# Latent mixer of a hybrid encoder step: search steps settled by GpSimd, and sixteen transposed copies moved from ACT to DVE

## What is computed

```python
def mla_core(k_nope, k_rope, v, k_pos, q_nope, q_rope, q_pos):        # mixer B
    logits = einsum('bqhd,bshd->bhqs', q_nope, k_nope) + einsum('bqhd,bsd->bhqs', q_rope, k_rope)
    logits = where(chunk_mask(q_pos, k_pos), logits * 96 ** -0.5, -inf)
    return einsum('bhqs,bshd->bqhd', softmax(logits, axis=-1), v)

idx_score = where(chunk_mask(q_pos, k_pos), idx_score, -inf)          # mixer A
_, sel = lax.top_k(idx_score, 256)
```

## Time and profile before

| | |
|---|---|
| median of three runs | 3007.67 us |
| the profiled execution, its own time | 3008.22 us |
| its span, first to last instruction | 3006.4 us |
| mean granted TensorE clock | 0.978 |
| PE busy over the span | 2833.9 us (94%) |
| DVE busy | 2018.3 us (67%) |
| ACT busy | 1412.2 us (47%) |
| POOL busy | 532.4 us (18%) |

### The profile page before, as it was taken

One profiled execution on the slowest core, in us unless ns is written; L12 is line 12 of the kernel. 1 busy time (PEld: TensorE's weight loads), 2 busy tenths in 40 slices (PEclk: granted clock), 3 DMA queues, 4 the chain that ended last, 5 costly groups with the idle time before them and its releaser, 6 DMA issues. The chain is left out here.

```text
span 3006.4 us, 49479 instructions
## 1 busy us (share of the span) xinstructions
PE 2833.9 (94%) x18462; PEld 2368.9 (79%) x18462; DVE 2018.3 (67%) x3648; ACT 1412.2 (47%) x2850; POOL 532.4 (18%) x410
## 2 busy tenths in 40 slices
PE   8986997999999999899999899999899999999998
PEld 6762564668899999788799566865688999998787
DVE  5447999865867776677631565139857777767777
ACT  5335996552444344433243455348724444444333
POOL 0000222420011110465000231000000111114551
PEclk9996999999999999999999999999999999999999
DMA  4111001021233323654411201120112333326442
GB/s 154 46 36 29 14 14 50 2 65 67 75 97 104 107 97 96 235 172 129 168 51 46 92 2 53 56 77 2 58 74 61 101 109 99 104 91 227 154 130 103
DMA packets 203120, 259.04 MB, mean 86 GB/s; under 512 B 27100, under 2 KB 132180, under 8 KB 202900
## 3 DMA queue, kind: packets, MB, share of 16 engines
q1 hardware_dynamic: 202900, 256.10, 25.8%
HBM read 177.90 MB, written 77.64 MB: 85 GB/s over the span
## 5 line engine op out<-in xcount | busy, mean ns | idle before, releaser
L247 PE MATMUL X<-up_th,high 128*128 128x272 f32 x1232 | 356.4, 289 | 4.1 <-ACT up_U L2287 2.9
L249 PE MATMUL X<-up_th,low_r 128*128 128x272 f32 x1232 | 355.2, 288 | 0.0
L247 PEld LDWEIGHTS X<-up_th,high 128*128 128x128 f32 x1232 | 232.2, 188 | 8.3 <-ACT up_U L2287 6.1
L2248 POOL TENSOR_TENSOR up_sum<-up_U 128x512 f32<-128x512 f32 x20 | 33.4, 1669 | 1131.9 <-DVE up_U L2399 1131.9
L249 PEld LDWEIGHTS X<-up_th,low_r 128*128 128x128 f32 x1232 | 231.9, 188 | 0.0
L2381 DVE SCALAR_TENSOR_TENSOR up_cv<-up_G,tap,up_cv 128x1024 f32<-128x1024 f32 (+1 forms) x176 | 130.3, 782 | 136.9 <-ACT up_cv L2296 135.3
L247 PE MATMUL up_x<-up_th,up_high 128*128 128x272 f32 x704 | 202.9, 288 | 1.4 <-DVE up_low_r L1859 1.4
L249 PE MATMUL up_x<-up_th,up_low_r 128*128 128x272 f32 x704 | 203.7, 289 | 0.0
L248 PE MATMUL X<-sums_r,high 128*128 128x272 f32 x528 | 152.0, 288 | 0.0
L247 PE MATMUL up_y<-up_th,up_high 128*128 128x272 f32 x528 | 151.9, 288 | 0.0
L249 PE MATMUL up_y<-up_th,up_low_r 128*128 128x272 f32 x528 | 151.6, 287 | 0.0
(11 more groups left out here) (581 smaller groups left out, 8665.6 us busy)
## 6 DMA issues: line engine op xcount, KB each, us to landing
scratch_a<-up_U SPq DMA_DIRECT2D x44, 544.0 KB, 2.7
low<-in_w_up_dram SPq DMA_DIRECT2D x44, 512.0 KB, 5.1
up_low<-in_w_up_dram SPq DMA_DIRECT2D x44, 512.0 KB, 4.9
scratch_s<-up_sum SPq DMA_DIRECT2D x80, 256.0 KB, 2.0
b_f<-in_w_down_dram SPq DMA_DIRECT2D x40, 512.0 KB, 4.4
a_lo_p_f<-scratch_s SPq DMA_DIRECT2D x40, 512.0 KB, 4.2
a_lo_p_f<-scratch_a SPq DMA_DIRECT2D x30, 512.0 KB, 4.5
scratch_att<-out_x SPq DMA_DIRECT2D x16, 512.0 KB, 2.6
```

Of the source, the lines that this page charges most:

```text
L247: nc.tensor.matmul(out, lh, rh, start=first, stop=False, skip_group_check=on_top)
L249: return nc.tensor.matmul(out, ll, rh, start=False, stop=last, skip_group_check=on_top)
L2248: g.tensor_tensor(t0, a21, a22, ALU.add).then_inc(pair_summed, 1)
```

## The change

Two edits in `attention`, for mixer B alone.

The settling moves from DVE to POOL. POOL's loop scales unit i for both heads and then settles the steps of unit i. It works with a difference and a signed step `flip` (a power of two whose sign is that of the score) in place of a comparison, a predicated copy and an exclusive-or. A step other than the first issues six operations: limit minus count; whether that is at least zero; that times `flip`; the sum of `bits` and the product; half of `flip`; the sum of the two as the next candidate. Each of the first three is waited for before the next. DVE's two calls of `settle` go; before `next_float` it waits for the last settling.

The copy of group 1 of head 1, `(x, j) == (1, 1)`, moves from ACT to DVE. Only wide units have a group 1, so there are 16 such copies, of 128, 256, 384 and 512 columns. On DVE they stand first in the unit.

```diff
--- before.py
+++ after.py
@@ -977,7 +977,9 @@
 
         if what == "x":
             return "dve" if j % 2 else "act"
-        if mla or stick:
+        if mla:
+            return "dve" if (x, j) == (1, 1) else "act"
+        if stick:
             return "act"
         return "act" if x == 0 else "dve"
 
@@ -995,7 +997,8 @@
             below = sb("below", [P, wide[-1]], BF16)
             up = sb("up", [P, n_top], mybir.dt.int32)
             counted = {"dve": sem("counted_dve"), "act": sem("counted_act")}
-            settled, cand_ready = sem("settled"), sem("cand_ready")
+            flip = sb("flip", [P, n_top], mybir.dt.int32)
+            settled, cand_ready, flipped = sem("settled"), sem("cand_ready"), sem("flipped")
         if mla or dsa:
             top, work, spare, told = src["top"], src["work"], src["top"]["spare"], sem("told")
             scratch = below if mla else sb("scratch", [P, 2 * SEQ], BF16)
@@ -1094,6 +1097,31 @@
                     for h in range(2):
                         g.memset(left[s][h][:, SEQ:SEQ + 1], 1.0).then_inc(cleared, 1)
                 return
+            def settle(step):
+
+                for by, n in (("dve", BY_DVE), ("act", n_top - BY_DVE)):
+                    pool.wait_ge(counted[by], FROM + n * (step + 1))
+                room = top["ok"][:].bitcast(F32)
+                g.tensor_tensor(room, top["limit"][:], top["cnt"][:], ALU.subtract).then_inc(settled, 1)
+                pool.wait_ge(settled, FROM + 4 * step + 1)
+                if step:
+                    g.tensor_scalar(top["cand"][:], room, 0.0, None, ALU.is_ge).then_inc(settled, 1)
+                    pool.wait_ge(settled, FROM + 4 * step + 2)
+                    g.tensor_tensor(top["cand"][:], top["cand"][:], flip[:], ALU.mult).then_inc(settled, 1)
+                    pool.wait_ge(settled, FROM + 4 * step + 3)
+                    g.tensor_tensor(top["bits"][:], top["bits"][:], top["cand"][:], ALU.add).then_inc(settled, 1)
+                    if step + 1 < STEPS:
+                        g.tensor_scalar(flip[:], flip[:], 0.5, None, ALU.mult).then_inc(flipped, 1)
+                else:
+                    g.tensor_scalar(top["bits"][:], room, 0.0, 1.0, ALU.is_ge, ALU.subtract).then_inc(settled, 2)
+                    g.tensor_scalar(flip[:], room, 0.0, 2.0, ALU.is_ge, ALU.mult).then_inc(settled, 1)
+                    pool.wait_ge(settled, FROM + 4)
+                    g.tensor_scalar(flip[:], flip[:], 1.0, float(1 << 30), ALU.subtract, ALU.mult).then_inc(flipped, 1)
+                if step + 1 < STEPS:
+                    pool.wait_ge(settled, FROM + 4 * step + 4)
+                    pool.wait_ge(flipped, FROM + step + 1)
+                    g.tensor_tensor(top["cand"][:], top["bits"][:], flip[:], ALU.add).then_inc(cand_ready, 1)
+
             for i, (p, t) in enumerate(order):
                 n, w = queries(t), key_tile(t)[0]
                 for h in range(2):
@@ -1101,6 +1129,8 @@
                     c = 2 * (i % ring) + h
                     pool.wait_ge(rcp_done[h], FROM + i + 1)
                     g.tensor_scalar(pr, pr, rr[0:n, c:c + 1], 1.0, ALU.mult, ALU.mult).then_inc(prob_ready[h], 1)
+                for step in (SEARCH_AT[i] if mla else ()):
+                    settle(step)
 
         @block.tensor
         def _(pe):
@@ -1417,20 +1447,6 @@
                     v_.tensor_scalar(below[:, wide[j]:wide[j + 1]], w[:], top["cand"][:, j:j + 1].bitcast(F32), None, ALU.is_lt, ALU.add,
                                      accum_out=top["cnt"][:, j:j + 1]).then_inc(counted["dve"], 1)
 
-            def settle(step):
-
-                for by, n in (("dve", BY_DVE), ("act", n_top - BY_DVE)):
-                    dve.wait_ge(counted[by], FROM + n * (step + 1))
-                v_.tensor_tensor(top["ok"][:], top["cnt"][:], top["limit"][:], ALU.is_le).then_inc(settled, 1)
-                dve.wait_ge(settled, FROM + 2 * step + 1)
-                if step:
-                    v_.copy_predicated(top["bits"][:], top["ok"][:], top["cand"][:]).then_inc(settled, 1)
-                else:
-                    v_.tensor_scalar(top["bits"][:], top["ok"][:], 1.0, None, ALU.subtract).then_inc(settled, 1)
-                dve.wait_ge(settled, FROM + 2 * step + 2)
-                if step + 1 < STEPS:
-                    v_.tensor_scalar(top["cand"][:], top["bits"][:], 1 << (30 - step), None, ALU.bitwise_xor).then_inc(cand_ready, 1)
-
             def not_above(columns):
                 for j in columns:
                     w = work[SEARCHED[j]]
@@ -1517,8 +1533,6 @@
                 if i + ahead < n_units:
                     for h in range(2):
                         peak(i + ahead, h)
-                if mla and len(SEARCH_AT[i]) > 1:
-                    settle(SEARCH_AT[i][0])
                 if i:
                     pieces_of(dve, "dve", i, "x")
                     if not mla:
@@ -1531,9 +1545,8 @@
                     count_below(SEARCH_AT[i][-1])
                 if i + 2 < n_units:
                     over_sum(i + 2, 0)
-                if mla and SEARCH_AT[i]:
-                    settle(SEARCH_AT[i][-1])
                 if mla and i == SEARCH_ENDS + 1:
+                    dve.wait_ge(settled, FROM + 4 * STEPS)
                     next_float()
                 if mla and i == SEARCH_ENDS + 2:
                     room_for_ties()
```

## The result

The changed kernel took 3219.31 us (median of 4 runs, 3214.08 to 3221.48), the kernel before 3008.07 beside it: a ratio of 1.0702 (95% interval 1.0683 to 1.072), **211.2 us slower**. The forecast was 3212 (3130 to 3280).

What follows compares the result with a forecast made beforehand. Before, DVE and ACT both full bound the search; the change closes a ring through POOL's queue. 3008.2 us plus 158 for the ring and 46 for PE's lower clock gave 3212 us, range 3130 to 3280.

Steps and rivals of the forecast that it cites:

- The bound of before: Mixer B's search, before: DVE and ACT both full, three counting passes each per step, 5.31 us a step, no visible chain.
- The queue on POOL: POOL's scaling of unit i+1 now stands behind settling unit i, which waits for the counts, making each step a closed ring.
- The length of the ring: Counts, settling, scaling, transposes, scores, peaks, counts in sequence: 10.7 us a step against 5.31, +158 us in all; clock separate.
- DVE's way: In the ring, ACT's way (copies, two exponentials, counts) is shorter by scores and peaks, so DVE's sets the length.
- The settling's price: Six small POOL operations and their waits per step: 2.4 us, from 1.2 low to 4.0 high.
- The intercept of the wide rows: POOL's wide two-operand operations leave 0.65 us at no columns, the upper estimate for each small two-operand one.
- The scores: PE's scores of the unit three on, one chunk of 512 columns in the ring: half of 2.82, 1.41 us.
- The clock: PE's pause of some 5 us per ring lowers its clock; transposes and first scores cost 1.6 us more, +46 us.
- The rival in which it stays up: PE's clock does not fall in the ring's pauses, so only the ring counts: 3166 us, chance 0.20.
- Nothing comes back behind the search: From 476 to 508 us DVE alone is full and its work is the same, so no time is regained.
- The copies: Sixteen copies moved from ACT to DVE, covered by waiting for PE's scores: costed at nothing, 10 us at most if uncovered.
- The rival with slack: The ring has slack, ACT sets the pace and loses twelve copies: at most 7 us less, 3001 us, chance 0.04.

## Why the prediction was right, step by step

- **The bound of before** held. That both engines are full means that relief of one buys nothing, and the run with the settling cut shows it.
- **The queue on POOL** was the step that decided, and two runs show it: the wait alone makes 159 us, and scaling one unit ahead takes 201 away.
- **The length of the ring** was forecast as 10.7 us and 1.6 for the clock, 12.3; over the 29 rings that hold one full unit, it is 12.38 on average (8.77 to 14.37). The two second steps of the doubled units, forecast to add 1 us each, took 4.52, which is 0.8 less than a step before. That DVE's way sets the length held in 26 of 32 steps; in the other 6 ACT's counts came last. By its links, from the starts on POOL's and DVE's timelines:

| link | predicted us | measured us |
|---|---|---|
| settling | 2.4 | 1.67 |
| two scalings | 1.58 | 1.38 |
| from there to the first peak: transposes, scores, wide units, clock | 0.78 + 1.41 + 0.3 + 1.6 = 4.09 | 4.54 |
| two peaks | 1.38 | 1.54 |
| key copy, counts, hand-over to POOL | 0.2 + 2.66 = 2.86 | 3.25 |
| sum | 12.3 | 12.38 |

So the sum is good partly because errors cancel: settling was put 0.7 us too long, 21 us over 29 rings, scaling 0.2 too long, while the other three links came out 0.45, 0.16 and 0.39 longer. That the search grew by 203 us where 204 were forecast is in that part luck.
- **The settling's price** failed by its middle value. Its lower half was right: four operations of 0.20 us, two of 0.25, and gaps of 0.3 us in all. The intercept of the wide rows (0.65 us) says nothing of a 6-column operation. The estimate by the 1.96 times of the Trainium skill, GPSIMD Engine Reference, "Performance versus the Vector engine", was 1.6; the trace has 1.67, but with six operations in place of three. Operation by operation the trace does not bear the ratio out at this size: POOL's two-tensor operation takes 0.20 us and DVE's comparison 0.166, 1.2 times as long.
- **The scores** were mis-sized. In the turn shown, DVE's first peak comes 4.77 us after PE begins them and not half of 2.82: a peak of 896 columns needs both chunks, and these ran largely at the low clock. The forecast also misread its row: the 2.82 us are four matmuls of 512 columns and four of 256, and the four of 512 take 1.79 of them (363.40 to 365.19 in the trace), not 1.41.
- **The clock** was put at 46 us. The two shapes on PE are 46.9 us longer, and busy filler gives back 38. That agrees with the mechanism; that 46.9 lies so near 46 is chance. The forecast took the transposes and the first chunk of each ring at 1.81/1.06 = 1.7 times their time; the 46.9 are all matmuls of the two shapes, which grew to 1.5 (907/604) and 1.4 (386/284) times. The exact share stays open, since the filler did not hold the clock up in all windows. The rival in which it stays up has fallen.
- **"Nothing comes back behind the search"** missed the other sign: 7.6 us are lost there. DVE's first peak behind the last step waits 6.89 us for the end of the last turn:

```profile
679.31 0.74 DVE L1447 TENSOR_SCALAR_CACHE_REDUCE att_b_below<-scores,top_cand 128x512 bf16<-128x512 f32 x1
...
687.09 1.09 DVE L1392 CUSTOM_DVE_ANT_0 att_b_prob<-att_b_s,att_b_hidden 128x896 f32<-128x896 f32 x1 [6.89 <-PE att_b_s L1158]
```

  The moved copies are no part of it: with the copies on ACT the same stretch is 42.4 us (664.69 to 707.09).
- **The copies** were costed at nothing, with 10 us as the most if the cover goes. The cover went in the ring: 12 us by the medians, 9 by the ratios, so whether 10 was the most is not settled. The 0.43 us a step between the two traces (11.87 less 11.44, 13 us in all) overstate it: they compare the slowest execution of the changed kernel with the fastest of the other.
- **The rival with slack** had at most 7 us to win. No run won it: neither the kernel with the settling cut nor those with 16 or 32 copies fewer on ACT came out below the kernel before.

What stays open: why the orders with two units ahead end at the time before or up to 5 us over it. ACT is busy for 151.6 to 155.7 of the same 160 us in them, where it had 158.5 before, so a full ACT alone does not explain it. Part of what it was relieved of comes back as waits for the next candidate, which POOL's settling now gives. In the order with 32 copies on DVE (300 to 512 us):

```profile
ACT att_b_below L1338 <- POOL top_cand L1123: 5.5, 9, 1.6
```

The kernel before has no such wait on ACT. No run separates these waits from the others.

## What to carry to other kernels

Before moving a waiting step to an idle engine, list what stands behind it in that engine's queue and ask whether it may run before the wait ends. If it feeds the work that ends the wait, the pipeline closes into a ring: here 0.46 us of settling, once POOL waited for it, cost 4.9 us a step, so faster operations alone would not have saved the change: with no work moved, 159 of the 211 us were still lost. And where two engines are both full, cut the work of one for a test before designing the move: here the time stayed, and there was no prize.

## What was not expected of the hardware

- POOL's operations on 128x6 take 0.20 us with two tensors and 0.25 with one and constants; on one column they follow each other every 0.145 us (0.87 for six). A settling of six, most of them each waiting for the one ahead, takes 1.67 us.
- Matmuls that nobody reads made the kernel 38 us faster, through the clock: the mean granted clock over the span rose from 0.945 to 0.970.
